# Three edits to the TensorE order of a two-block transformer kernel: a modulation unit placed later, GLA outputs head by head, query sums as columns

## The reference

```python
for l in range(DEPTH):
    shift, scale, gate = jnp.split(c_act @ w_ada[l] + b_ada[l], 3, axis=-1)
    h = rms_norm(x, norm_w[l]) * (1.0 + scale[:, None, :]) + shift[:, None, :]
    (gq, gk, gv, glr, gz, dq, dk, dv, da, db, dz, aq, ak, av, az) = jnp.split(h @ w_in[l], bounds, axis=-1)
    ...
    o_gla = gla_chunked(...)        # chunks of 64: o = att @ v  +  q_e @ s_prev
    ...
    q_d = rms_norm(aq.reshape(B, S, DIFF_HEADS, 2, DIFF_D), diff_q_norm_w[l]).transpose(0, 2, 3, 1, 4)
    k_d = rms_norm(ak.reshape(B, S, DIFF_HEADS, 2, DIFF_D), diff_k_norm_w[l]).transpose(0, 2, 3, 1, 4)
    q_d = apply_rope(q_d, cos_b, sin_b)
    ...
    y = jnp.concatenate([o_gla, o_gdn, o_diff], axis=-1) @ w_out[l]
    x = x + gate[:, None, :] * y
```

## Time and profile before

| | |
|---|---|
| median of 3 runs | 2866.85 us (2865.04 to 2868.89) |
| the profiled execution | 2866.85 us, its span 2865.0 us |
| TensorE matmul | 94% of the span |
| VectorE, GpSimd, ScalarE | 61%, 52%, 42% |
| chain that ended last | TensorE 76%, VectorE 12%, DMA 5%, ScalarE 3% |
| line 2389, the products | 57% of the chain |
| granted TensorE clock | 0.97 over the run |

### The profile page before, as it was taken

How to read it: one execution, slowest core, us unless ns; L and a number is a source line. 1 busy time by engine, 2 the same in 40 slices (tenths; PEclk the granted TensorE clock), 3 DMA queues, 4 the chain that set the end, 5 groups by cost and what they waited for, 6 DMA issues and landing times.

```text
span 2865.0 us, 51222 instructions
## 1 busy us (share of the span) xinstructions
PE 2705.7 (94%) x22151; PEld 2504.8 (87%) x22151; DVE 1745.1 (61%) x1905; ACT 1206.9 (42%) x1438; POOL 1489.3 (52%) x1071
## 2 busy tenths in 40 slices
PE   5799999999999999999999969899999898999999
PEld 2489999888888899989989959899899798999999
DVE  2344444654555658786677656964866668745653
ACT  1233444333443334444576354533453445434542
POOL 0056766986666787776445826544547755400000
PEclk9699999999999999999999979999999999999999
DMA  9999998998887997776546837755658776644555
GB/s 338 287 313 263 269 266 248 291 277 258 241 235 227 288 254 222 212 208 182 162 133 183 235 84 211 204 154 158 173 159 217 197 196 180 162 113 123 132 155 154
DMA packets 948768, 599.21 MB, mean 209 GB/s; under 512 B 22070, under 2 KB 945088, under 8 KB 948032
## 3 DMA queue, kind: packets, MB, share of 16 engines
q1 hardware_dynamic: 944720, 582.83, 72.7%
q10 hardware_dynamic: 3824, 13.11, 1.2%
HBM read 589.46 MB, written 6.29 MB: 208 GB/s over the span
## 4 chain that ended last, share of the span: by engine, by line
PE 76%; DVE 12%; DMA 5%; ACT 3%; issue 2%; SPq 1%; DVEq 0%; ACTq 0%
PE G L2389 57%; DMA ring<-in_w_mod_dram 3%; DVE ring_r L1462 3%; PE A L2329 2%; DMA const<-in_w_mod_dram 2%; DVE S L2220 1%; PE A L2449 1%; PE A L2455 1%; PE A L2452 1%; PE G L2471 1%; PE A L2490 1%; SPq L714 1%; ACT ring_r L863 1%; PE G L2827 1%; PE A L2839 1%
## 5 line engine op out<-in xcount | busy, mean ns | idle before, releaser
L2389 PE MATMUL G<-H_r,ring_r 128*128 128x256 f32 x10032 | 1704.6, 287 | 59.2 <-DVE S_r L1451 21.5
L2389 PEld LDWEIGHTS G<-H_r,ring_r 128*128 128x128 f32 x10032 | 1475.9, 192 | 92.1 <-issue 63.6
L820 POOL TENSOR_TENSOR ring<-ring,act_in 128x512 f32<-128x512 f32 x448 | 689.7, 1559 | 950.1 <-DMA ring<-in_w_ada_dram 710.2
L1462 DVE TENSOR_TENSOR ring_r<-ring,ring_r 128x2048 fp32r<-128x2048 f32 x346 | 865.9, 2503 | 279.5 <-ACT ring_r L863 278.5
L863 ACT ACTIVATE ring_r<-ring 128x2048 fp32r<-128x2048 f32 x346 | 661.6, 1912 | 319.2 <-PE G L2389 105.0
L2389 PE MATMUL G<-M_r,ring_r 128*128 128x256 f32 x4528 | 789.6, 284 | 0.0
L2389 PEld LDWEIGHTS G<-M_r,ring_r 128*128 128x128 f32 x4528 | 645.5, 190 | 9.2 <-issue 8.6
L2389 PE MATMUL G<-S_r,ring_r 128*128 128x256 f32 x1920 | 548.4, 286 | 0.0
L2389 PEld LDWEIGHTS G<-S_r,ring_r 128*128 128x128 f32 x1920 | 371.9, 194 | 3.4 <-issue 3.4
L823 POOL TENSOR_TENSOR ring<-ring 128x512 f32<-128x512 f32 x224 | 346.3, 1546 | 17.6
L829 POOL TENSOR_TENSOR ring<-ring 128x256 f32<-128x256 f32 x168 | 204.2, 1216 | 13.2
(11 more groups left out here) (441 smaller groups left out, 2559.4 us busy)
## 6 DMA issues: line engine op xcount, KB each, us to landing
ring<-in_w_in_dram SPq DMA_DIRECT2D x120, 1024.0 KB, 5.7
ring<-in_a_w_in_dram SPq DMA_DIRECT2D x98, 1024.0 KB, 6.6
ring<-in_w_ada_dram SPq DMA_DIRECT2D x192, 512.0 KB, 6.8
const<-in_w_mod_dram SPq DMA_DIRECT2D x192, 256.0 KB, 5.2
ring<-in_c_w_in_dram SPq DMA_DIRECT2D x48, 1024.0 KB, 5.9
ring<-in_w_mod_dram SPq DMA_DIRECT2D x16, 2048.0 KB, 18.0
ring<-in_a_w_out_dram SPq DMA_DIRECT2D x32, 1024.0 KB, 6.6
ring<-in_w_out_dram SPq DMA_DIRECT2D x32, 1024.0 KB, 5.9
```

Source lines behind the costliest of these rows:

```text
L820: g.mark(pool.tensor_tensor(w[:, i:i + 2, :], w[:, i:i + 2, :], act_in[:, k:k + 2, c:c + 1].broadcast_to((P, 2, BW)), ALU.mult))
L1462: v.tensor_tensor(w_low(tl), w_raw(tl), w_up(tl).bitcast(F32), ALU.subtract).then_inc(w_lo, 1)
L2389: ins = pe.matmul(G[tl.bank][:, 0:SEQ], w, x, start=(k == 0 and n_ == 0), stop=(k == KT - 1 and n_ == 2))
```

## The change

It has three parts.

1. The units of a tile are cut in two: the first two of `GEMV_AT[q]` stay in `after_first_half`, what is left (one unit in 16 tiles) runs behind the tile's second half.
2. The GLA outputs are formed one head at a time, all four chunks of a head in a row.
3. The sums of the queries' squares are formed as columns: 16 matmuls whose weights are 128x128 squares and whose moving operand is one column of ones, straight into 16 columns of G3. The two transposes and VectorE's copy go, and the scaling, the root and the reciprocal of the queries work on 16 columns in place of 256. The keys stay as they were.

```diff
@@ act, mixers
-                    take_root(f"diff_q{l}", df["q_rows"])
+                    take_root(f"diff_q{l}", small[:, 32:48])
@@ dve, mixers
-                    q_rows = df["q_rows"]
-                    ask_root(f"diff_q{l}", q_rows, G[3][:, 0:SEQ], 1.0 / P)
-                    V(v.reciprocal(q_rows, q_rows))
-                    V(v.tensor_scalar(q_rows, q_rows, P ** -0.5, None, ALU.mult))
+                    ask_root(f"diff_q{l}", small[:, 32:48], G[3][:, 0:16], 1.0 / P)
+                    V(v.reciprocal(small[:, 32:48], small[:, 32:48]))
+                    V(v.tensor_scalar(small[:, 32:48], small[:, 32:48], P ** -0.5, None, ALU.mult))
...
-                    turned_q = G[3][:, SEQ:2 * SEQ].rearrange("p (t g x) -> p t g x", t=2, g=4)
-                    V(v.tensor_copy(small[:, 32:48].rearrange("p (t g r) -> p t g r", t=2, g=4), turned_q[:, :, :, 0:2]))
@@ pe, after_first_half
-                gemv_units(GEMV_AT.get(q, ()))
+                gemv_units(GEMV_AT.get(q, [])[0:2])
@@ pe, product
                         if half == 0:
                             after_first_half(q)
+                        else:
+                            gemv_units(GEMV_AT.get(q, [])[2:])
@@ pe, mixers, gla_o
-                    for p in range(2):
-                        for t in range(2):
-                            for b in range(2):
-                                h = 2 * p + b
+                    for h in range(GLA_H):
+                        p, b, o = h // 2, h % 2, 64 * (h % 2)
+                        for c in range(NCH):
+                            t = c // 2
+                            if c % 2 == 0:
                                 pe.matmul(G[2 + b][...], GV[...], gla["att"][...], start=True, stop=False, ...)
-                            for c in range(max(1, 2 * t), 2 * t + 2):
-                                for b in range(2):
-                                    o = 64 * b
-                                    ins = pe.matmul(G[2 + b][...], gla["st"][...], qe[...], start=False, stop=True, ...)
+                            if c:
+                                ins = pe.matmul(G[2 + b][...], gla["st"][...], qe[...], start=False, stop=True, ...)
@@ pe, mixers, diff_qs and diff_bc
-                    ins = row_sums(None, [(j // 2, j % 2, df["sq_q"][:, j, :]) for j in (0, 2, 4, 6, 1, 3, 5, 7)], G[3], SEQ)
+                    for j in range(8):
+                        for t in range(2):
+                            ins = pe.matmul(G[3][:, t * 8 + j:t * 8 + j + 1], df["sq_q"][:, j, t * P:(t + 1) * P], ones[:, 0:1],
+                                            start=(j == 0 and t == 0), stop=True, skip_group_check=True)
...
-                    for t in range(2):
-                        pe.transpose(G[3][:, SEQ + t * P:SEQ + (t + 1) * P], df["q_rows"][:, t * P:(t + 1) * P], ident)
```

More of the change, by code:

```diff
@@ L651, in build @@
               "sq_k": M[:, 4096:6144].rearrange("p (j t) -> p j t", j=8), "rows8": S[:, 5120:5376],
-              "q_rows": S[:, 5376:5632],
               "P": [two(S[:, 0:512]), two(S[:, 512:1024])], "PT": [E[:, 0:256], E[:, 256:512]],
@@ L2754, in mixers @@
                                           skip_group_check=True)
-                            for c in range(max(1, 2 * t), 2 * t + 2):
-                                for b in range(2):
-                                    o = 64 * b
-                                    ins = pe.matmul(G[2 + b][:, p * SEQ + c * CHUNK:p * SEQ + (c + 1) * CHUNK],
-                                                    gla["st"][o:o + 64, c - 1, p * P:(p + 1) * P],
-                                                    qe[o:o + 64, p, c * CHUNK:(c + 1) * CHUNK], start=False, stop=True,
-                                                    skip_group_check=True)
+                            if c:
+                                ins = pe.matmul(G[2 + b][:, p * SEQ + c * CHUNK:p * SEQ + (c + 1) * CHUNK],
+                                                gla["st"][o:o + 64, c - 1, p * P:(p + 1) * P],
+                                                qe[o:o + 64, p, c * CHUNK:(c + 1) * CHUNK], start=False, stop=True,
+                                                skip_group_check=True)
                     PS.done(ins, "gla_o")
```

## The result

The changed kernel takes 2894.88 us (median of 5; 2884.96 to 2896.65) against 2866.85; the ratio on record, over more executions, is 1.0092, 95% interval 1.0077 to 1.0107, so some +26 us where +10.9 was forecast. The direction was right, the size was not: 2894.88 lies far above the range of 2871 to 2883. The profiled execution is one of the shorter ones: 2885.66 us, span 2882.8.

What follows compares the result with a forecast made beforehand. The prediction took TensorE, busy 94% of the span, to bound the kernel. Its terms 3.9 + 5.4 + 1.6 = +10.9 us on 2866.85 gave 2877.8 us, with a range of 2871 to 2883 for 8 in 10.

Steps and rivals of the forecast that it cites:

- Part 2: GLA outputs, both layers: more shape turns and no side-by-side row groups, about 7.1 us against 4.39, +5.4 us in all.
- Part 3: Query sums, both layers: 3.6 us of one-column matmuls; -0.3 us in the first layer, +1.9 in the second, +1.6.
- both waits: TensorE's waits for the key rows' root before the broadcast, 1.74 and 0.41 us, were to go.
- Part 1: Third modulation unit of 16 tiles, half a tile later: an extra shape turn, +3.9 us in all.
- starved tiles: Tiles 8, 9, 52 and 53, where weights from DMA are late: moving the third unit was taken to cost 0.
- Rival 3: At the four tiles short of weights, SyncE's queue blocks and loads come up to 2.8 us later: 2889.1 us, 8%.
- Rival 1: At boundaries between full and tiled matmuls, shape turns are hidden: +2.0 us in all, 2868.8 us, 8%.
- Rival 2: Behind the GLA outputs, later waits swallow their 5.4 us shift: 2872.4 us, 9%.
- Rival 4: All 11.2 us of waits for modulation weights go, with the moved units' price: faster, 2862.6 us, 3%.
- a free lone unit: Sign of being wrong: the lone modulation unit adds nothing, where about 0.76 us more between two starts was expected.
- less idleness of VectorE: Sign of being wrong: VectorE's 7.26 us idleness before the GLA row sums shrinks by 2.7 us.
- new waits for DMA: Sign of being wrong: new waits for DMA stand at tiles 8 to 60.

Runs made afterwards that it cites:

- e2: Kernel before with only the GLA outputs changed, formed head by head: ratio 1.0045 (1.0028 to 1.0063), +13 us.
- e4: Kernel before with the GLA outputs grouped, all 128-row matmuls, then all 64-row ones side by side (part of the sums lost): ratio 0.9996.
- e7: Kernel before with GLA outputs head by head, each head's two 128-row matmuls first, then its three 64-row ones: ratio 1.0011, +3 us.
- e8: Kernel before with only the query sums changed, as 16 matmuls with 128 moving columns in place of one: ratio 1.0028, +8 us.
- e3: Kernel before with only the query sums changed, as 16 matmuls with one moving column: ratio 1.0026 (1.0012 to 1.0040), +7.5 us.
- e5: Kernel before with all but the first modulation unit moved behind the second half in all 88 tiles with units: ratio 1.0175, +50 us.
- e1: Kernel before with only the third modulation unit of 16 tiles moved half a tile later: ratio 1.0031 (1.0020 to 1.0041), +9 us.
- e6: Kernel before with matmuls in place, only the third unit's signal in 16 tiles given at the second half's end: ratio 1.0011, +3 us.
- e18: Kernel before with GLA outputs grouped by shape (two turns) and the gated delta rule's step-ending matmuls likewise (one turn): ratio 0.9972, -8 us.
- e9: Kernel before with two of 24 pairs of small modulation matmuls issued twice, 0.9 us of added rows: ratio 1.0025, +7 us.

## Why the prediction was too small

- **Part 2, +5.4.** This is the step that failed. "GLA outputs: about 7.1 us" holds to 0.1 us for the matmuls at full clock (7.02). What failed is the silent assumption that the clock stays at the full level, as it does in all the rows from which the prices came: the layer paid 5.6 us, not 2.7, +11 in all in the profile, +13 measured (e2). Of the 16 turns' cost, e4 and e7 part it: half is turns, half the lost overlap of row groups, and of the two only the turns were seen to bring the clock down. With the old order the clock fell in 0 of the 20 profiled stretches, with 8 turns and no overlap in 0 of 4, with 12 in 1 of 2, with 16 in 6 of 6.
- **Part 3, +1.6.** 3.6 us for the sums is right, and so is the end of both waits. At full clock (e8) TensorE comes to the broadcast 0.63 and 1.96 us later than before, as forecast (0.6 and 1.9). The same assumption on the clock failed here: the key sums and the first part of the next tile ran at half clock, in 8 of 8 profiled stretches with one column, in 0 of 2 with 128, which adds 1.4 us (e3; up to 3 in the changed kernel). In the first layer the rotation's wait swallows nearly all of it, as forecast in kind: over eight tiles the five profiles with part 3 take 70.1 to 70.9 us, the 15 without it 67.1 to 71.1, a mean of 0.5 more where -0.3 was forecast. In the second layer they take 66.9 to 70.0 against 63.5 to 65.0, a mean of 4.0 more where 1.9 was forecast. Together +4.5 in the profiles; measured +7.5, with an interval from 3.4.
- **Part 1, +3.9.** The term was right by its rows: 3.6 us in the 12 tiles, a lone unit as long as a pair, nothing at the starved tiles. Measured +9 (6 to 12) and, without the starved tiles, +6 (2 to 9). The surplus does not grow with the units moved (e5), and e1's mean clock doesn't carry it. The delayed signal is not shown to cost anything (e6), nor quite excluded. 2 to 5 us of part 1 stay open.
- **The rivals.** None came true. Rival 3 (weights later) has nearly the size but not the mechanism: waits for modulation weights grew by 1.7 us. Rivals 1, 2 and 4 are refuted: a turn costs 0.14 to 0.17, the GLA shift stays whole, and the waits for weights did not go.
- **The sum.** The profiles place 3.6 + 11.3 + 4.5 = 19.4 us. That is 8.5 above the forecast: 5.9 in part 2, all of it half clock in and behind the GLA outputs, and 2.9 in part 3, most of it half clock, less 0.3 in part 1. Measured were +26 (22 to 31) and +21 (16 to 26). The means of all executions agree: of +23 us (2891.6 against 2868.4), 17 us more at the half level (within 7) give up to 8, and 15 are left for work and waits at full clock, against 10.9 forecast. So about two thirds of the miss is the clock; the rest, some 4 us, is not placed by the profiles and not far above the scatter.
- **The range.** It had no end for a loss of clock, though the kernel before showed half-clock stretches elsewhere, one of them behind the same alternation (the first of the second layer's three). None of the prediction's own signs of being wrong (a free lone unit, less idleness of VectorE, new waits for DMA) asked for the clock, and none of them showed.

## What to carry to other kernels

A price read from rows holds at the clock of those rows. If a change makes TensorE alternate tile shapes for microseconds, or feed it one column per weight load, look in the profile for the granted clock behind the places that already do so, and give the range an end at half clock there, product behind it included. A single profiled execution can be quick or slow by 3 to 4 us in a stretch that nobody changed, so lay several profiles side by side before you call a difference the change's. And order small matmuls by shape: all of one, then all of the other, was worth 0.3% here (e18, 0.2 to 0.4).

## What was unexpected of the hardware

- TensorE was busy without a gap and its clock still fell to 1.2 GHz: some 5 us into the changed GLA outputs (16 turns), and at the end of 3.6 to 4 us of one-column matmuls, where as many matmuls per microsecond with 128 columns kept it in both layers. The Trainium skill ("TensorE: Matmul & The Clock Gate", HAM oscillation) tells of idle gaps between bursts of matmuls as what brings the low clock back. The trace agrees for other falls: behind the wait of 2.9 us for the rotation in the first layer the kernel before ran at a granted clock of 0.50 for 6 us. It doesn't agree here, where TensorE never stood idle, and the measurement decides.
- The fall reaches into dense work: the 24 product records behind such a stretch took up to 5.05 us from the first start to the last (e9), in place of 2.7.
- Behind 64-row singles in turn with full ones the clock falls or doesn't: at 0 to 6 of 6 places in kernels that are identical there. Two kernels whose rows differ by 0.9 us were 7 us apart (e9; 4 to 11).
- A lone modulation unit costs as much as a pair: 0.76 us from product record to product record, against 0.77 (e5 and the kernel before).
